# Two chained transformer blocks on one core: 25 convolution taps moved ahead of the first attention, its turned probabilities copied by ScalarE, and the heads' half of the output projection issued first

## The reference: what is computed

```
u = val * sigmoid(gate)                               # 512 channels, from h @ w_in
dw = causal depthwise convolution of u, 31 taps, + conv_b
y_conv = silu(layer_norm(dw))
q = rms_norm(c_q) @ w_q_b;  kv = rms_norm(c_kv) @ w_kv_b     # 8 heads, latents c_q, c_kv from h @ w_in
q, k: rms_norm and rotation; p = softmax(q k^T * scale, chunk mask); y_attn = p v
x = x + g_a * (concatenate([y_conv, y_attn]) @ w_out)
x = x + g_f * mixture_of_experts(norm(x))             # 32 experts, top 2
```

## Time and profile before

| | |
|---|---|
| three runs, median (range) | 2281.28 us (2277.46 to 2281.7) |
| the profiled execution: its time, its span | 2281.54 us, 2279.8 us |
| TensorE busy | 2037.2 us (89%) |
| VectorE busy | 1141.1 us (50%) |
| ScalarE busy | 712.3 us (31%) |
| GpSimd busy | 165.5 us (7%) |
| mean granted TensorE clock | 0.944 of full speed |
| first attention loop on PE, from its first filler to the last iteration's end | 211.93 to 291.69 us |

### The profile page before, as it was taken

The page is one execution under the profiler, slowest core; times in us unless marked ns, Lnnn a source line. Parts: engine busy times, 40 slices in busy tenths (PEclk is TensorE's granted clock), DMA queues, the critical chain, the costliest instruction groups (busy, mean ns, idle before and its releaser), DMA issues.

```text
span 2279.8 us, 25908 instructions
## 1 busy us (share of the span) xinstructions
PE 2037.2 (89%) x8901; PEld 1461.5 (64%) x8901; DVE 1141.1 (50%) x1833; ACT 712.3 (31%) x1186; POOL 165.5 (7%) x175
## 2 busy tenths in 40 slices
PE   3997888189999599899999999999989999999995
PEld 2445545166666355775678887875678467888784
DVE  2658932378878549663432223353875433222235
ACT  1032221055555222452223332213145223333221
POOL 2000000313333100000000000010000000000001
PEclk8997998599999798899999999998999999999998
DMA  9152011469998530002213333231000222335220
GB/s 355 53 221 77 1 74 75 146 235 365 352 359 343 216 117 1 20 2 102 56 56 95 107 106 107 94 132 75 1 20 2 101 56 74 92 92 153 69 92 37
DMA packets 149438, 269.43 MB, mean 118 GB/s; under 512 B 12144, under 2 KB 109600, under 8 KB 136160
## 3 DMA queue, kind: packets, MB, share of 16 engines
q1 hardware_dynamic: 142496, 258.46, 32.0%
q0 software_dynamic: 6848, 9.77, 1.4%
HBM read 257.64 MB, written 23.14 MB: 123 GB/s over the span
## 4 chain that ended last, share of the span: by engine, by line
PE 76%; DVE 14%; issue 3%; DMA 3%; ACT 2%; POOL 1%; SPq 0%; DVEq 0%; ACTq 0%; POOLq 0%
PE bank L234 14%; PE bank L236 14%; PE bank L235 14%; PE bank L2243 5%; PE bank L2088 5%; PE bank L2132 4%; PE bank L2023 3%; PE bank L1928 2%; DVE arena L1732 2%; PE bank L2204 2%; DVE arena L1731 2%; PE bank L2215 2%; DMA arena<-w_ada 1%; PE bank L2185 1%; PE bank L1904 1%
## 5 line engine op out<-in xcount | busy, mean ns | idle before, releaser
L234 PE MATMUL bank<-ht_hi,gate_up_hi 128*128 128x512 f32 x704 | 274.1, 389 | 2.9 <-ACT arena L1276 2.9
L235 PE MATMUL bank<-ht_lo,gate_up_hi 128*128 128x512 f32 x704 | 273.9, 389 | 0.0
L236 PE MATMUL bank<-ht_hi,gate_up_lo 128*128 128x512 f32 x704 | 273.9, 389 | 0.0
L2132 PE MATMUL bank<-arena 128*128 128x512 f32 (+3 forms) x640 | 202.5, 479 | 8.1 <-ACT arena L1169 7.3
L2132 PEld LDWEIGHTS bank<-arena 128*128 128x128 f32 x640 | 120.3, 206 | 87.2 <-issue 76.6
L1569 DVE TENSOR_TENSOR expert_gate_up_lo<-expert_gate_up,expert_gate_up_hi 128x2048 fp32r<-128x2048 f32 x64 | 146.6, 2293 | 58.2 <-ACT expert_gate_up_hi L1096 58.2
L1809 DVE TENSOR_TENSOR arena<-arena,bank 128x512 f32 (+1 forms) x44 | 30.3, 688 | 272.1 <-ACT arena L1188 272.1
L234 PEld LDWEIGHTS bank<-ht_hi,gate_up_hi 128*128 128x128 f32 x704 | 132.2, 188 | 30.8 <-issue 3.8
L236 PEld LDWEIGHTS bank<-ht_hi,gate_up_lo 128*128 128x128 f32 x704 | 132.2, 188 | 27.6
L235 PEld LDWEIGHTS bank<-ht_lo,gate_up_hi 128*128 128x128 f32 x704 | 132.2, 188 | 27.4
L1096 ACT CAST expert_gate_up_hi<-expert_gate_up 128x2048 fp32r<-128x2048 f32 x64 | 121.6, 1902 | 73.6 <-PE bank L236 73.4
(11 more groups left out here) (326 smaller groups left out, 3526.4 us busy)
## 6 DMA issues: line engine op xcount, KB each, us to landing
gate_up_whole<-w_gu SPq DMA_DIRECT2D x88, 512.0 KB, 5.1
expert_gate_up<-w_gate_e SPq DMA_DIRECT2D x32, 1024.0 KB, 6.9
expert_gate_up<-w_up_e SPq DMA_DIRECT2D x32, 1024.0 KB, 9.7
arena<-w_down_e SPq DMA_DIRECT2D x32, 1024.0 KB
down_whole<-w_down SPq DMA_DIRECT2D x44, 512.0 KB, 3.5
arena<-w_ada SPq DMA_DIRECT2D x5, 4096.0 KB, 22.3
arena<-w_in SPq DMA_DIRECT2D x4, 2048.0 KB, 14.7
arena<-w_o SPq DMA_DIRECT2D x2, 4096.0 KB, 13.0
```

The lines of the kernel that those rows point to most:

```text
L234: pe.matmul(ps, xh, wh, start=start, stop=False)
L235: pe.matmul(ps, xh, wl, start=False, stop=False)
L236: return pe.matmul(ps, xl, wh, start=False, stop=stop)
L2132: ins = pe.matmul(ps[:, 0:b - a], HT[:, c, t * P:(t + 1) * P], w_in2[j][:, c], start=c == 0, stop=c == C8 - 1)
```

## The change

The tap table grows: 82 taps instead of 62 stand behind the fourth input block, so 20 more run before DVE's wait for the latents' roots, and five more (`HEAD_TAPS` 87) stand behind DVE's copies of the transposed latents. The loop keeps 37 of its 62 taps: none in tile 0, one an iteration in tile 1, two in tiles 2 and 3. `take_pt` moves from DVE to ACT, where the copy of n - 3 stands ahead of the exponential of n, and the last three copies stand behind the loop. `mix` is split: the heads' four matmuls of piece (0, 0) go between `mean` and `var`, those of (0, 1) and (1, 0) behind `var`, then the convolution's four of each of these three, then the other five pieces with all eight.

```diff
-EARLY_TAPS = (0, 15, 30, 46, 62)
+EARLY_TAPS = (0, 15, 30, 46, 82)
+HEAD_TAPS = 87
...
     b.take(("mean",))
+    b.take(("mix", 0, 0))
     b.take(("var",))
     for t in range(T):
-        for half in range(2):
+        for half in range(t == 0, 2):
             b.take(("mix", t, half))
...
+            def take_pt(n):
+                t, h = divmod(n, NH)
+                if n >= 3:
+                    weighted(act, n - 3)
+                ps = u1.read(act, ("pT", t, h))
+                u1.free(act.copy(PT[:, n % 3, 0:(t + 1) * P], ps[:, 0:(t + 1) * P]), ("pT", t, h))
+
             n = 0
             for t in range(T):
                 for h in range(NH):
                     w = (t + 1) * P
+                    if n >= 3:
+                        take_pt(n - 3)
                     act.wait_ge(s_negmax, n + 1)
-                    if n >= 3:
-                        u1.evacuated(act, ("pT",) + divmod(n - 3, NH))
...
+            for n in range(T * NH - 3, T * NH):
+                take_pt(n)
...
+            for k in range(EARLY_TAPS[MC], HEAD_TAPS):
+                conv(k // TAPS, k % TAPS)
+            own.settle()
...
+            k = HEAD_TAPS
             for n in range(T * NH + 3):
                 if n < T * NH:
                     row_max(n)
-                for k in (2 * n, 2 * n + 1):
-                    if k < 2 * TAPS:
-                        conv(2 + k // TAPS, k % TAPS)
-                if 2 <= n < T * NH + 2:
-                    take_pt(n - 2)
+                for _ in range((0, 1, 2, 2)[min(n // NH, T - 1)]):
+                    if k < MC * TAPS:
+                        conv(k // TAPS, k % TAPS)
+                        k += 1
...
+            pe.wait_ge(s_wout, 64)
+            for j in range(4):
+                u1.evacuated(pe, ("oT", j))
+
+            def mix(t, half, ms):
+                ps = u1.begin(pe, ("mix", t, half)) if ms[0] else bank[u1.b.where[("mix", t, half)][0]]
+                for m in ms:
+                    if m == 0:
+                        pe.wait_ge(s_yconv, MC)
+                    ins = pe.matmul(ps[:], mixT[:, m, t * P:(t + 1) * P], w_out[:, m, 512 * half:512 * half + 512],
+                                    start=m == MC, stop=m == MC - 1)
+                if m == MC - 1:
+                    u1.full(ins, ("mix", t, half))
+
+            heads, convs = range(MC, C8), range(MC)
+            mix(0, 0, heads)
             ps = u1.begin(pe, ("var",))
...
+            mix(0, 1, heads)
+            mix(1, 0, heads)
+            for half in range(2):
+                mix(0, half, convs)
+            mix(1, 0, convs)
+            mix(1, 1, [*heads, *convs])
+            for t in range(2, T):
                 for half in range(2):
-                    ps = u1.begin(pe, ("mix", t, half))
...
+                    mix(t, half, [*heads, *convs])
```

More of the change, by code:

```diff
@@ L709, in width, with weighted @@
             return min(t + 1, 2) * P if kind == "a" else (t + 1) * P
+        def weighted(eng, n):
+            t, h = divmod(n, NH)
+            if h == NH - 1:
+                u1.read(eng, ("o", t))
+            else:
+                eng.wait_ge(s_pv, t * (NH - 1) + h + 1)
         def weighted2(eng, n, l):
@@ L1414, in _ @@
                 u1.free(dve.tensor_copy(KT[0:QK, h], ps[0:QK, :]), ("kT", h))
[L1416 to L1422, removed]
             def row_max(n):
@@ L1428, in row_max @@
                 dve.tensor_scalar(nmx[:, t, h:h + 1], mx[:, t, h:h + 1], -(QK ** -0.5), None, ALU.mult).then_inc(s_negmax, 1)
[L1430 to L1435, removed]
             def take_o(t):
```

## The result

The changed kernel takes **2249.81 us** (median of 4 runs, 2248.5 to 2253.04) where the one before takes 2280.26 on the same chip (4 runs, 2277.46 to 2281.7). The ratio is 0.9869, with a 95% interval of 0.9853 to 0.9885: some 30 us less, and 26 to 34 by the interval. The profiled execution took 2249.24 us, with a span of 2247.5 and a mean clock of 0.949.

A forecast was written before the change was run, and what follows sets the result against it. The prediction took DVE to set the pace in three of the loop's four tiles, with PE standing still before `mix`. It summed 2281.5 + 1.6 (head) - 17 (loop) - 10.5 (projection) to 2256 us, range 2250.5 to 2264.

The forecast's parts named there:

- What bounds the kernel: DVE sets the pace in three of the loop's four tiles; in the projection PE stands still 7.99 us before `mix`.
- The loop: First attention's loop: shorter iterations from moved taps and copies, forecast at -17 us, bounds -12 and -19.
- the floors' -18.0: Loop's four stretches and drain (-5.7, -7.8, -3.0, -2.1, +0.6) priced at full clock without friction where an engine changes: 18.0 us gained.
- The end: Loop's drain: ACT's copy of 29 stands behind the exponential of 31, costing +0.6 us.
- POOL beside the taps: Head, at the latents' roots: POOL's small instructions and the last taps delay each other, +1.6 us, bounds 0 and +1.9.
- The rival of a falling clock: Clock falls in the shorter loop too, costing 4.9 us, and the projection's 2.1 aren't won: 2262.6; chance 16%.
- The projection: Heads' matmuls fill PE's waits: `var` +1.9, 52 matmuls left of 64 -10.3, clock -2.1, together -10.5 us.
- The clock part of it: In the projection, the low clock in the first 9 us behind PE's standstill goes too: -2.1 us.
- The lower end of the range: Whole kernel: head 0, loop -19, projection -10.7, then 1.5 for runs below the median: 2250.5 us.
- the pace of the hand-overs: Rival in the loop: a late maximum delays ACT's copy, 0.25 us an iteration, 8 us: 2263.6; chance 10%.
- the table's swapping: Rival in the loop: ACT swaps its table between copy and exponential, +39 us, so 2312; chance 2%.
- the taps hide fully beside POOL: Rival at the head: the taps cost +0 there, giving 2254 us; chance 8%.

The follow-up runs named there:

- e1: The kernel before with only the 25 taps moved, DVE still copying and the projection as before; 2265.43 us, ratio 0.9948.
- e2: The kernel before with only `take_pt` moved to ACT, two taps in every iteration as before; 2267.51 us, ratio 0.9951.
- before again: The kernel before, unchanged, run once more for a second profile; 2275.11 us in one run.
- e6: The changed kernel with 17 taps, not 20, ahead of the latents' roots and the three others at the loop's end; 2246.63 us, ratio 0.986.
- e5: The changed kernel without its 25 moved taps, so ACT's copy and the split projection alone; 2257.35 us, ratio 0.9901.
- e12: The changed kernel with 17 taps ahead of the latents' roots, two heads' matmuls before `var` and ten behind, one filler an iteration instead of two; 2244.92 us.
- e8: The changed kernel with 12 filler matmuls on PE ahead of its wait for the scaled latents; 2252.88 us, ratio 0.9889.

## Why the prediction came out as it did

**What bounds the kernel: right.** DVE set the pace in tiles 0 to 2. Taking taps away shortened tiles 0 and 1 (e1), taking the copies away tiles 2 and 3 (e2), and of the exposed 7.99 us in the projection 1.08 are left.

**The loop: the step that failed, by its size.** The term was -17, cut from the floors' -18.0 for friction; it measured -20.5 (tiles -6.53, -8.15, -3.37 and -3.01, end +0.56, by the end of PE's work). The end and the order of what limits each tile came as forecast. The prediction had the same fall of the clock in tile 1 before it and said that it cost little; before again shows it to be worth 1.5 us, so a loop without it gives 19.0. Three sizes in the term were wrong.
- PE's floor in tile 3 was priced at 2.75 us, with 0.96 for `values` from a group behind the last mask. A full iteration is 262.00 to 264.64, so 2.64, and in it the eight records of `values` take 0.84 us, from 263.80 to the next filler. The starts on PE (duration second, with the pipeline's end in it):

```profile
262.00 0.59 PE L1978 MATMUL bank<-arena 128*128 128x512 bf16 x2
262.44 1.02 PE L1979 MATMUL bank<-arena 96*128 96x512 f32 x2
263.30 0.22 PE L1980 MATMUL bank<-arena 128*128 128x128 bf16 x1
...
263.80 1.00 PE L1992 MATMUL bank<-arena 128*128 128x64 f32 x8
264.64 0.59 PE L1978 MATMUL bank<-arena 128*128 128x512 bf16 x2
```

- The exponential and its accumulator were added, 0.37 + 0.19. On ACT they overlap with what follows; from start to start it is 0.35. With it two iterations of tile 0 take 2.37 us (1.00 and 1.37 from scores to scores) and not 2.53. ACT's timeline in tile 0:

```profile
216.09 0.37 ACT L1078 ACTIVATE arena<-bank,arena 128x128 f32<-128x128 f32 x1
...
216.44 0.36 ACT L1078 ACTIVATE arena<-bank,arena 128x128 f32<-128x128 f32 x1
...
216.79 0.37 ACT L1078 ACTIVATE arena<-bank,arena 128x128 f32<-128x128 f32 x1
...
217.13 0.27 ACT L1068 COPY arena<-bank 128x128 f32<-128x128 f32 x1
```

- No friction showed. PE is busy 12.47 of 12.50 and 20.18 of 20.18 us in tiles 1 and 3, so the hand-overs between engines were hidden there. The allowance of 1 us was for nothing that the trace of before had shown.

ACT's copy is not free everywhere: tile 0 is 7.91 us with DVE's copy (e1) and 8.65 with ACT's, presumably since there the copy stands in line with the exponentials (argued, not tested). In tiles 2 and 3 it gives more than that back.

**POOL beside the taps: the mechanism right, the size half.** +1.6 was taken, 0.84 came (bounds 0 and 1.9). The forecast had taps and POOL take turns and delay each other. In the trace only POOL waits: the nineteen taps keep their 0.785 us (14.93 in all). They end 1.54 us behind POOL's first start, where 2.1 had been reckoned, also because one of the twenty is a scaling of 0.54 us. POOL's first instruction runs its 0.19 us; the second and third meet a tap each and are stretched by 0.33 and 0.51. The columns show that the 0.84 us is passed on whole. The Trainium skill, "SBUF — State Buffer", section "Who interferes with whom", has the rule that a two-input DVE instruction and a GpSimd instruction reading SBUF exclude each other; the trace agrees, with 0.52 and 1.53 us in the changed kernel against 0.19 and 1.02 in e6.

**What was missed: the clock behind the latents**, 2.4 us. The rival of a falling clock was placed in the loop and in the projection, where it didn't happen; the prediction did not look at PE's wait ahead of the q and kv projections, which the hold-up lengthens from 2.66 to 3.50 us. In 4 of 4 profiles with 3.50 us the clock fell behind it; with 2.66 it held in seven and fell in two (e5, e12); with 0.80 it held (e8). The price is the same in each: from the scaling to the transposes of q and k it is 54.23 to 54.25 us in the eight profiles in which the clock held, with or without the hold-up, and 56.6 to 56.8 in the six others. So the longer wait makes the fall far likelier and isn't its only condition. What else decides in e5 and e12, and behind the loop, where a wait of some 1.1 us was enough in 4 of 14 profiles, stays open.

**The projection: right.** `var` starts 3.43 us behind `mean` (forecast 3.4), the wait is 1.08 (1.4), the last piece 44.90 (some 45), together -10.6 for -10.5. The clock part of it was right as well: no stretch of the last piece is at the lower level, and its 104 records are 0.432 us each, where the earlier trace rows have 57.10 us for 128, or 0.446. Against before again it would be -12.0, of which 1.6 are its transposes at the lower level.

**The sum.** Head +3.2 for +1.6, loop -20.5 for -17, projection -10.6 for -10.5: -27.9 for -25.9. The two errors had opposite signs, and half of the larger was cancelled, which is luck. The changed kernel's profile is 6.4 us below the 2255.6 of the sum: 2.0 of that are these terms, and the other 4.4 are the stages that no edit touches, which move by some 3 us each between executions. The profile that the sum started from was near the slow end of its kernel's runs (2281.54 of 2277.46 to 2281.7). So the terms that failed explain a third of the miss, and the spread of the unchanged stages, which the range allowed 1.5 us for, the rest. The lower end of the range took -19 for the loop, which was no bound: it was made from the same floor. It was also added up wrongly by 0.2: 2251.8 less 1.5 is 2250.3, not 2250.5.

Of the rivals, the falling clock in the loop, the pace of the hand-overs and the table's swapping are refuted by the clock of 1.00 in all four tiles, by PE's full tiles and by the loop's single table load at 214.79. That the taps hide fully beside POOL is refuted by its 3.48 us, which go back to 2.65 in e6.

## What to carry to other kernels

Read an engine's floor from a stretch in which it waits for nothing, and from start to start, not by adding records: both errors here made the gain look smaller than it was. When work is put into an engine's wait, see who else works in that wait (POOL's four small instructions here) and how long PE then stands still, since its clock may fall for part of the next stage: here 0.84 us of hold-up cost 3.2. Take a second profile of the kernel before ahead of the forecast: it would have shown which stretches of the first were a matter of chance. And when two edits ease the same engine, price them together, for alone they win partly the same time.

## What the runs showed of the hardware

- Between executions, untouched stages moved by some 3 us each way (115.3 to 118.3 us to (a), 1896.9 to 1900.4 behind h2T in eleven of the twelve rows above).
- Nineteen two-source DVE instructions kept their 0.785 us while POOL's small instructions beside them were stretched from 0.19 and 1.02 to 0.52 and 1.53 us: here POOL did the waiting.
- The granted clock fell behind PE waits of 3.50 us in 4 of 4 profiles, of 2.66 us in 2 of 9, of 0.80 us in 0 of 1, and elsewhere behind one of some 1.1 us in 4 of 14. At the latents a fall cost 2.4 to 2.6 us, behind the loop 1.6.
- Without fillers the clock was 0.50 for eight microseconds in tiles 0 and 1 and 1.00 in tiles 2 and 3; with one of 0.21 us an iteration it stayed at 1.00. That is one profile of each.
- In the one profile with twelve matmuls added inside a wait, PE stopped for 4.77 us some 1350 us later, where the profile has no releaser for it.
